# Feed-forward tiles taken from the unscaled residual, and eight filler tiles moved in the last delta rule head

## The reference

```python
for i in range(DEPTH):                        # DEPTH = 2
    h = rmsnorm(x, norm_mix_w[i])
    out = hybrid_mixer(h) if i % 2 == 0 else ssm_mixer(h)
    x = x + out
    h = rmsnorm(x, norm_ffn_w[i])             # x * rsqrt(mean(x*x) + EPS) * w
    x = x + (silu(h @ wg) * (h @ wu)) @ wd    # D_FF = 2816
y = rmsnorm(x, norm_final_w)
```

## Time and profile before

| | us |
|---|---|
| median of 3 runs | 3410.31 (3408.43 to 3412.93) |
| time of the profiled execution | 3412.15 |
| its span | 3410.4 |
| chain that ended last: PE, DVE, ACT | 82%, 12%, 3% of the span |
| PE busy | 3202.9 (94%) |
| DVE busy | 1589.0 (47%) |
| POOL busy | 999.5 (29%) |
| ACT busy | 782.5 (23%) |

### The profile page before, as it was taken

One profiled execution on the slowest core, in us unless ns is written; L12 is line 12 of the kernel. 1 busy time (PEld: TensorE's weight loads), 2 busy tenths in 40 slices (PEclk: granted clock), 3 DMA queues, 4 the chain that ended last, 5 costly groups with the idle time before them and its releaser, 6 DMA issues.

```text
span 3410.4 us, 46632 instructions
## 1 busy us (share of the span) xinstructions
PE 3202.9 (94%) x20050; PEld 3073.6 (90%) x20050; DVE 1589.0 (47%) x1899; ACT 782.5 (23%) x1115; POOL 999.5 (29%) x528
## 2 busy tenths in 40 slices
PE   6999989999899999999988999999978999999997
PEld 5898888888789999999987898989967999999997
DVE  5343656565542222222286867778586312221224
ACT  4212334223330000000044414243244100000002
POOL 2222201111023333333223535344351323232321
PEclk9999999999899999999999999999998999999998
DMA  4111101101011111111112213122230111111111
GB/s 143 64 56 64 48 19 39 32 32 39 14 43 44 50 44 50 44 50 44 44 41 78 96 56 120 56 101 78 73 111 25 48 50 45 49 44 50 47 47 62
DMA packets 79241, 190.79 MB, mean 56 GB/s; under 512 B 20901, under 2 KB 36933, under 8 KB 78921
## 3 DMA queue, kind: packets, MB, share of 16 engines
q1 hardware_dynamic: 52384, 150.03, 13.1%
q10 hardware_dynamic: 26664, 37.88, 3.6%
HBM read 164.07 MB, written 19.59 MB: 54 GB/s over the span
## 4 chain that ended last, share of the span: by engine, by line
PE 82%; DVE 12%; ACT 3%; issue 2%; DMA 1%; ACTq 0%; SPq 0%; DVEq 0%
PE ps_set L546 67%; PE ps_core L819 4%; PE ps_set L555 3%; ACT work L1079 2%; DVE work L1594 2%; PE ps_core L1014 1%; ACT L1079 1%; DVE work L1918 1%; DVE h_lo L1580 1%; DVE work L1802 1%; PE ps_core L1019 1%; DVE work L2129 1%; PE ps_set L630 1%; PE ps_core L1009 1%; DVE work L2081 1%
## 5 line engine op out<-in xcount | busy, mean ns | idle before, releaser
L472 POOL CAST w_hi<-w_raw 128x1024 fp32r<-128x1024 f32 x230 | 255.3, 1110 | 2230.5 <-PE ps_set L546 1993.4
L546 PE MATMUL ps_set<-h_hi,w_hi 128*128 128x344 f32 x3696 | 815.1, 329 | 13.9 <-ACT work L1079 13.8
L546 PE MATMUL ps_set<-h_lo,w_hi 128*128 128x344 f32 x3696 | 786.6, 321 | 0.0
L546 PE MATMUL ps_set<-h_hi,w_lo 128*128 128x344 f32 x3696 | 782.9, 320 | 0.0
L546 PEld LDWEIGHTS ps_set<-h_hi,w_hi 128*128 128x128 f32 x3696 | 622.6, 189 | 37.5 <-issue 17.5
L546 PEld LDWEIGHTS ps_set<-h_lo,w_hi 128*128 128x128 f32 x3696 | 627.1, 189 | 0.0
L546 PEld LDWEIGHTS ps_set<-h_hi,w_lo 128*128 128x128 f32 x3696 | 618.6, 188 | 0.0
L475 POOL TENSOR_TENSOR w_lo<-w_raw,w_hi 128x1024 fp32r<-128x1024 f32 x230 | 595.5, 2589 | 18.4
L2016 DVE TENSOR_TENSOR work<-work,ps_set 128x1032 f32<-128x1032 f32 x44 | 54.1, 1229 | 816.2 <-PE ps_set L546 806.3
L1669 DVE TENSOR_TENSOR x<-x,ps_set 128x1032 f32<-128x1032 f32 x160 | 196.7, 1229 | 256.4 <-PE ps_set L546 256.4
L1079 ACT ACTIVATE work<-ps_set 128x1032 f32<-128x1032 f32 x116 | 120.1, 1035 | 751.4 <-PE ps_set L546 721.0
(11 more groups left out here) (219 smaller groups left out, 3447.9 us busy)
## 6 DMA issues: line engine op xcount, KB each, us to landing
w_raw<-in_w SPq DMA_DIRECT2D x230, 512.0 KB, 3.3
work<-ssm_cum_rows ACTq DMA_DIRECT2D x32, 512.0 KB, 4.1
sample<-in_ssm_state SPq DMA_DIRECT2D x16, 512.0 KB, 4.1
out_ssm_s<-sample SPq DMA_DIRECT2D x16, 512.0 KB, 2.6
x<-in_x SPq DMA_DIRECT2D x6, 688.0 KB, 14.8
work<-work ACTq DMA_DIRECT2D x16, 258.0 KB, 2.4
out_y<-x SPq DMA_DIRECT2D x6, 688.0 KB, 3.4
sample<-bc_rows SPq DMA_DIRECT2D x8, 512.0 KB, 5.0
```

What stands on the lines that cost most here:

```text
L472: return nc.gpsimd.tensor_copy(w_hi[:, k, :], w_raw[:, k, :])
L546: mm = nc.tensor.matmul(out[:, g, 0:TN], w[:, slot, cols], v[:, g * TN:(g + 1) * TN], start=(start and n == 0), stop=(stop and n == 2))
```

## The change

At boundaries 1 and 3 the feed-forward tiles are fed with x * w without the root. ACT rounds x * w to h_hi straight from x (`products`), DVE makes h_lo from x, w and h_hi in one instruction (`lows`). The root is made once for all tokens (three logarithms, one exponential, RSTD) and is applied by DVE after the matmuls: the gate product times RSTD from PSUM (`gate`, written to SBUF), then silu on ACT from SBUF, then silu times RSTD (again DVE), then times the up product. So each tile A and B has two more DVE instructions of 1032 columns, and the gate's PSUM set is read by DVE, no more by ACT. At boundary 1 all twelve adds to x come first, then `lows` and `sums`; at boundary 3 they are interleaved. PE runs the mean squares between the projections.

Tile B is handled by token groups on DVE and ACT (`gated_b`, `hi_b`). For the last pair PE also makes ub group by group (`by_group`), and the output tiles of group g wait only for y_lo of that group.

In the last delta rule head one filler tile stays after kt, one is put ahead of the wait for Nb, six go into chunks 0 to 5 of the scan; the adds move with them.

```diff
@@ PE, boundary
-                def projections(g):
-                    for jobs, job, unit in first:
+                def projections(g, between=lambda: None):
+                    for k, (jobs, job, unit) in enumerate(first):
+                        if k:
+                            between()
...
+                if n in (1, 3):
+                    for g in range(TG):
+                        outputs_of(g)
+                    projections(0)
+                    mean_square(0)
+                    projections(1)
+                    mean_square(1)
+                    projections(2, lambda: mean_square(2))
+                    return
@@ PE, gated_delta
                 batch("s", K, Q, gdn_dve.value(n("qn")))
-                fill(out, 1)
+                if h + 1 < HEADS:
+                    fill(out, 1)
...
-                fill(out, 1)
+                fill(out, 0 if h + 1 == HEADS else 1)
+
+                late = h + 1 == HEADS
...
                     if lv > 1:
-                        fill(out, 1)
+                        if not late:
+                            fill(out, 1)
                         decode(lv)
...
+                if late:
+                    fill(out, 1)
                 pe.wait_ge(*gdn_dve.value(n("Nb")))
...
                     fill(ahead, 2)
-                    if h + 1 == HEADS and c == 4:
+                    if late and c < 6:
+                        fill(out, 1)
+                    if late and c == 4:
                         gdn_rms(h, 0)
@@ PE, ffn
+                def by_group(jobs, job, turn, unit):
+                    part = take(jobs, job, turn)
+                    pe.wait_ge(w_split, unit + 1)
+                    for g in range(TG):
+                        for c in range(KC):
+                            mm = group_products(ps_set[part][:, g, :], unit % 2, c, (h_hi[:, c, :], h_lo[:, c, :]), g,
+                                                c == 0, c == KC - 1)
+                        mm.then_inc(*((unit_done, 1) if g == TG - 1 else (part_done, 1)))
...
             def ffn_outputs(m, base, g):
                 unit = base + 6 * PAIRS - 2
+                pe.wait_ge(*ffn_dve[m].value(f"loB{g}", PAIRS - 1))
                 for q in range(4):
                     if g == 0 and q % 2 == 0:
-                        pe.wait_ge(*ffn_dve[m].value("loB", PAIRS - 1))
@@ ACT, boundary
+                def products(g, first=0, last=KC):
+                    for c in range(first, last):
+                        if c % 2 == 0:
+                            act.wait_ge(*x_pair_ready(n, g, c // 2))
+                        fn(h_hi[:, c, span(g)], x[:, c, span(g)], ACT.Identity, scale=NORM_W[:, n, c:c + 1])\
+                            .then_inc(*norm_act[n].step(f"hi{c}.{g}"))
...
+                    if n == 1:
+                        products(0)
+                        products(1)
+                        squares(0)
+                        products(2)
+                    else:
+                        products(0, 0, 4)
+                        products(1, 0, 4)
+                        products(0, 4)
+                        products(2, 0, 4)
+                        products(1, 4)
+                        products(2, 4)
+                        squares(0)
+                    squares(1)
+                    squares(2)
...
+                    for g in range(TG):
+                        logs(g)
+                    for g in range(TG):
+                        act.wait_ge(*core.read(f"ms{g}"))
+                    fn(RSTD, RSTD, ACT.Exp, scale=-0.5).then_inc(*norm_act[n].step("rstd"))
@@ ACT, ffn
-                    fn(grp(tok(c)), big(jobs.part(gate)), ACT.Silu).then_inc(jobs.sem(gate), 1)
+                    act.wait_ge(*jobs.read(gate, turn))
+                    fn(tok(c), tok(c), ACT.Silu).then_inc(*ffn_act[m].step("silu" + "AB"[c]))
@@ DVE, boundary
+                def lows(g, first, last):
+                    for c in range(first, last):
+                        dve.wait_ge(*norm_act[n].value(f"hi{c}.{g}"))
+                        v.scalar_tensor_tensor(h_lo[:, c, span(g)], x[:, c, span(g)], NORM_W[:, n, c:c + 1],
+                                               h_hi[:, c, span(g)].bitcast(F32), ALU.mult, ALU.subtract)\
+                            .then_inc(*norm_dve[n].step(f"lo{c}.{g}"))
...
+                if n == 1:
+                    for g in range(TG):
+                        for q in range(4):
+                            add(g, q)
+                    lows(0, 0, KC)
+                    lows(1, 0, KC)
+                    sums(0)
+                    lows(2, 0, KC)
+                    sums(1)
+                    sums(2)
+                    return
+                if n == 3:
+                    lows(0, 0, 4)
+                    for g in range(TG):
+                        add(g, 2)
+                        if g + 1 < TG:
+                            lows(g + 1, 0, 4)
+                        lows(g, 4, 6)
+                        add(g, 3)
+                        lows(g, 6, 8)
+                    for g in range(TG):
+                        sums(g)
+                    return
@@ DVE, gated_delta
-                add_before(1)
+                if not last:
+                    add_before(1)
...
-                add_before(2)
+                if not last:
+                    add_before(2)
...
-                        if m == "N" and lv > 1:
+                        if m == "N" and lv > 1 and not last:
                             add_before(lv + 1)
...
+                if last:
+                    add_before(1)
...
+                    if last and c < 6:
+                        add_before(c + 2)
@@ DVE, ffn
+                def gate(jobs, name, turn, unit, c, pair, before):
                     dve.wait_ge(unit_done, unit + 1)
...
+                    v.tensor_tensor(grp(tok(c)), grp(RSTD), big(jobs.part(name)), ALU.mult).then_inc(jobs.sem(name), 1)
+                    dve.wait_ge(*ffn_act[m].value("silu" + "AB"[c], pair))
+                    v.tensor_tensor(tok(c), tok(c), RSTD, ALU.mult).then_inc(*ffn_dve[m].step("f" + "AB"[c]))
...
+                def gated_b(jobs, up, turn, unit, pair, last=False):
...
+                    for g in range(TG):
+                        if last and g < TG - 1:
+                            dve.wait_ge(part_done, parts + (PAIRS - 1) * 6 + g + 1)
+                        else:
+                            dve.wait_ge(unit_done, unit + 1)
+                        v.tensor_tensor(tok(3)[:, span(g)], tok(1)[:, span(g)], ps_set[jobs.part(up)][:, g, 0:TN], ALU.mult)\
+                            .then_inc(*((jobs.sem(up), 1) if g == TG - 1 else ffn_dve[m].step(f"gB{g}")))
+                        if g:
+                            low(g - 1)
+                    low(TG - 1)
```

130 lines of the change are left out of this document (83 added, 47 removed).

## The result

The changed kernel takes 3387.90 us (3385.32 to 3391.47, four runs) against 3411.47 us (3408.43 to 3412.93, four runs) of the kernel before in the same session. The ratio is 0.9935 with a 95% interval of 0.9922 to 0.9948, so it is faster, by 0.65%. The forecast was 3384.8 with a range of 3373 to 3395. The profiled execution took 3387.24 with a span of 3385.5: 24.9 us less than before.

What follows compares the result with a forecast made beforehand. TensorE was taken to bound the kernel, with only its waits at the boundaries and in the last head movable: 11.4 + 8.8 + 6.5 - 1.2 = 25.5 us off 3410.31 gave 3384.8; range 3380 to 3390, with A and B 3373 to 3395.

Steps and rivals of the forecast that it cites:

- Feed-forward part, 0: Inside the feed-forward parts: TensorE's 11.37 us per tile cover VectorE's and ScalarE's longer chain, so cost 0.
- Boundaries 2 and 4, 11.4: After each feed-forward part: the wait for y_lo and the low clock behind it go, gaining 6.0 and 5.4 us.
- the wait that takes the old one's place: Boundaries 2 and 4: GpSimd's subtraction delays VectorE's third lower part, the addition queues behind it; 1.2 us charged each.
- Boundary 1, 8.8: Between last delta rule head and first feed-forward part: gb starts at 971.4 instead of 980.16, gaining 8.8 us.
- 18.7: Boundaries 1 and 3: the time in us from sum 0 to gb.
- Boundary 3, 6.5 (5.1 to 7.5): Ahead of the second feed-forward part: gb at 2647.1, or 2649.5 with low clock, instead of 2654.55; 6.5 us taken.
- 2.1 for one split: Boundary 3: of two units GpSimd splits there, one was charged as holding VectorE's lower parts, by 2.1 us.
- The last head, -1.2: Last delta rule head: moving filler saves 7.6 us before the scan, costs 9.6 in it, 0.8 back; net -1.2.
- A: Rival, chance 0.25: GpSimd and VectorE hardly meet, every charged hold is given back, 9.4 us in all, so 3375.
- B: Rival, chance 0.18: TensorE's pauses before mean square 0 cost 6.3 us more at one boundary, scan at -3.8; 3395.
- C: Rival, chance 0.06: the boundaries' own chain isn't shortened, as RSTD waits for all three sums anyway; 3400.
- D: Rival, chance 0.03: VectorE's longer chain makes TensorE wait in each feed-forward pair turn; slower, 3438 at two holds.

Runs made afterwards that it cites:

- gate_four: The changed kernel with three more VectorE multiplications ahead of each second gate product, into a tile nobody reads; 3390.44 us, ratio to before 0.9937.
- late_low: The changed kernel with the last pair's third groupwise lower part behind the first two output additions on VectorE, at boundaries 2 and 4; 3387.61 us, ratio to before 0.9926.
- all_wait: The changed kernel, but the first output group after each feed-forward part waits for y_lo of all three groups, as before; 3397.65 us, ratio to before 0.9958.
- b3_adds: The changed kernel with VectorE adding both jobs of a group together at boundary 3, and ScalarE squaring group 0 before later products; 3380.57 us, ratio to before 0.9911.
- ms_later: The changed kernel with TensorE's mean square of group 0 moved behind the projections of group 1 at boundary 3; 3384.65 us, ratio to before 0.9922.
- changed_again: The changed kernel run once more without any edit; 3388.33 us.
- head_alone: The kernel before with only the move of the last head's fill from its levels to its scan; 3412.01 us, ratio to before 1.0001.
- combo_b1: The changed kernel with b3_adds, late_low, the last head's additions one chunk later, and four lower parts ahead of boundary 1's last two additions; 3372.66 us, ratio to before 0.9887.

## Why the prediction was right, and where it was off

- **Feed-forward part, 0**: measured 0. gate_four shows that the cover is at least four products deep.
- **Boundaries 2 and 4, 11.4**: measured 6.2 and 5.3, in all 11.5, with the 0.37 that the account books under the feed-forward parts. The step on the wait that takes the old one's place was right in place and size: 1.2 charged, 1.32 measured, and late_low removed it by the cause named. all_wait shows the rest: the first output job's wait for the whole y_lo, and the clock behind it.
- **Boundary 1, 8.8**: measured 9.05, in the repeats 8.5 to 8.8. Inside it two deviations cancel: sum 0 came at 950.3 instead of 952.7, of which 1.3 is TensorE's earlier resumption and 1.1 the boundary's own, and from there to gb it took 19.5 instead of 18.7.
- **Boundary 3, 6.5 (5.1 to 7.5)**: measured 3.1. This is the term that was mis-sized. The step "2.1 for one split" failed: both of GpSimd's splits met VectorE, 4.3 us by the three rows shown, and sum 0 came 39.2 us after the start of the output jobs instead of 37.4. The 2.1 was also too low for one split, as it left out the 0.86 of the L1660 row of the kernel before. From sum 0 to gb it took 21.2 instead of 18.7. Of these 2.5, the low clock behind the pause is 1.6 (10.41 from the first mean square to the second, where boundary 1 at a clock of 1.00 took 8.77); I had put it down as the bound and charged part of it. The other 0.8 is missing from the 18.7 itself, at boundary 1 as well. From the 7.5 that held one split and no low clock, 1.8 and 2.5 leave 3.2. How large the second split's share is can't be read off more finely, since the order of VectorE also decides what its queue has to catch up. b3_adds and ms_later show that this isn't a price of the new arithmetic: another order on the same engines gives back 9.0 or 4.3.
- **The last head, -1.2**: measured -1.7 in the first profile, about -1.0 by the repeats. The chunk of 3.7 was right (3.65, five times); the levels' 38.64 were 39.46 and in changed_again 38.65, and the difference is the X1 batch's clock.
- **The sum, 25.5**: the medians give 23.6, the spans 24.9, of which 2.96 lie ahead of everything that was changed. Without those it is 22.0, 3.5 under the forecast, and boundary 3 is nearly all of it. The forecast's base less 22.0 would be 3388.3, still inside the range, so the range was met without them; that the spans' 24.9 stands so near to 25.5 is luck. The start of head 3 differs by up to 5 us in these fourteen profiles.
- **Rivals**: A (GpSimd and VectorE hardly meet) is refuted by L2157's 3.71 and L1686's 3.26. B (pauses cost more) happened in part, at boundary 3. C (the boundaries' own chain isn't shortened) is refuted by the 9.05; its mechanism shows as gb's wait of 0.66 for the gate, no more. D is refuted by gate_four.

For the hold the prediction drew on the Trainium skill (SBUF — State Buffer, "Who interferes with whom"), by which a VectorE instruction contends with a GpSimd instruction that reads SBUF when it has two SBUF inputs itself, and not when it has one. The trace agrees: two of L2157 together took 2.6 us longer beside L480 and L483, two of L1686 2.2, and the addition with PSUM as one input kept its 0.87 in late_low.

## What to carry to other kernels

When work moves onto an engine that others wait for, look for the order of that engine's queue rather than its sum: VectorE took 87 us more in a feed-forward part, and 79 more on top, without any loss of time, while the order of six additions, 24 lower parts and three sums at one boundary (with ScalarE's order to match) was worth 9 us. Put filler where it shortens a pause of TensorE, and take its consumer one step later than its producer, so that neither stands in the chain. Compare profiles piece by piece between fixed instructions: most pieces repeated to 0.4 us where whole times of one kernel lay 2 to 9 apart, and a difference that lies ahead of the first edit isn't the edit's.

## What the hardware showed that I had not expected

- The same pause, in the same code, is followed by a lower granted clock in some executions and not in others: behind the pause of 2.07 us ahead of head 3 the mean over 6 us was 0.78 in one profile and 1.00 in another, and the stretch took 29.1 or 27.5 us. Behind the pause of 1.32 us at boundary 2 it stayed at 1.00, and B2 repeats at 16.74 to 16.76 in every profile that has it; a lower clock followed each of the six of 4.17 to 4.75 us (before, head_alone, all_wait), with means of 0.50 to 0.64 over the 3.5 to 5.5 us behind them. The length of the pause doesn't settle it: behind 1.89 us at boundary 1 of combo_b1 the clock was 0.51 for 2.6 us, and behind 2.42 us at boundary 3 of the changed kernel it was 1.00.
- The 48 matmuls of X1 took 8.70, 7.46 or 5.99 us. The first two are the same kernel behind the same pause of 3.54, the third stands behind one of 2.57.
- GpSimd's subtraction also becomes longer when VectorE meets it (2.40 in the earlier trace rows, 2.92 at 2596.68), so both sides pay.
